# Relative bias added by VectorE in the band attention, and a new order of work around the second block's attentions

## The reference

```python
q = (u @ w_q).reshape(bsz, n_chunks, CHUNK, B_HEADS, B_HEAD_DIM)...
rel = jnp.clip(k_pos[None, :] - q_pos, -REL_CLIP, CHUNK - 1) + REL_CLIP
bias = rel_bias.astype(jnp.float32)[rel].transpose(2, 0, 1)
s = jnp.einsum('bqhd,bkhd->bhqk', qc, kb).astype(jnp.float32) * scale + bias
s = jnp.where(valid, s, MASK_VALUE)
p = jax.nn.softmax(s, axis=-1).astype(vb.dtype)
return jnp.einsum('bhqk,bkhd->bqhd', p, vb)
```

## Time and profile before

| | us |
|---|---|
| median of 3 runs | 1487.49 |
| lowest, highest | 1486.2, 1488.25 |
| profiled execution, its time | 1483.92 |
| profiled execution, its span | 1481.9 |
| PE busy | 1437.8 (97%) |
| DVE busy | 755.2 (51%) |
| ACT busy | 565.2 (38%) |

### The profile page before, as it was taken

How to read it: one execution, slowest core, us unless ns; L and a number is a source line. 1 busy time by engine, 2 the same in 40 slices (tenths; PEclk the granted TensorE clock), 3 DMA queues, 4 the chain that set the end, 5 groups by cost and what they waited for, 6 DMA issues and landing times. The chain is left out here.

```text
span 1481.9 us, 26323 instructions
## 1 busy us (share of the span) xinstructions
PE 1437.8 (97%) x11240; PEld 1211.5 (82%) x11240; DVE 755.2 (51%) x1194; ACT 565.2 (38%) x885; POOL 28.6 (2%) x47
## 2 busy tenths in 40 slices
PE   7999999999999999999999899999999999999997
PEld 4998899999999879999999789888666566566664
DVE  3968767876776656555555655644122122122121
ACT  2522235343454555444444664451212212212211
POOL 0100000000001010000000000010000000000000
PEclk9999999999999999999999999999999999999999
DMA  9996455979769514665645336426999999999996
GB/s 370 309 322 211 155 174 196 328 279 319 280 225 327 177 52 164 207 222 204 210 132 168 118 114 236 163 62 253 413 424 427 425 427 425 428 427 425 426 425 263
DMA packets 155378, 404.14 MB, mean 273 GB/s; under 512 B 5107, under 2 KB 123152, under 8 KB 133906
## 3 DMA queue, kind: packets, MB, share of 16 engines
q1 hardware_dynamic: 152960, 396.90, 71.1%
q0 software_dynamic: 1648, 5.18, 1.2%
q10 hardware_dynamic: 674, 0.64, 0.1%
HBM read 401.63 MB, written 1.07 MB: 272 GB/s over the span
## 5 line engine op out<-in xcount | busy, mean ns | idle before, releaser
L1999 PE MATMUL ps<-u,wsplit 128*128 128x256 f32 x3744 | 461.7, 284 | 5.3 <-DVE wsplit L1268 5.3
L1999 PEld LDWEIGHTS ps<-u,wsplit 128*128 128x128 f32 x3744 | 452.8, 192 | 11.9 <-DVE wsplit L1268 6.4
L1268 DVE TENSOR_TENSOR wsplit<-arena,wsplit 128x1024 fp32r<-128x1024 f32 x258 | 312.5, 1226 | 198.7 <-ACT wsplit L807 198.5
L807 ACT ACTIVATE wsplit<-arena 128x1024 fp32r<-128x1024 f32 x258 | 270.1, 1056 | 294.9 <-PE ps L1999 150.8
L2666 PE MATMUL ps<-arena 128*64 128x256 f32 x1408 | 155.9, 379 | 1.1 <-DVE arena L1897 0.8
L2666 PEld LDWEIGHTS ps<-arena 128*64 128x64 f32 x1408 | 101.6, 137 | 60.8 <-issue 12.6
L1902 DVE TENSOR_TENSOR arena<-arena,ps 128x256 f32<-128x256 f32 x32 | 13.5, 422 | 235.9 <-ACT arena L1216 223.8
L2261 PE MATMUL ps<-hid,wsplit 128*128 128x256 f32 x1056 | 130.7, 283 | 0.3 <-DVE hid L1524 0.3
L2261 PEld LDWEIGHTS ps<-hid,wsplit 128*128 128x128 f32 x1056 | 128.3, 192 | 0.5 <-DVE hid L1524 0.5
L1221 ACT ACTIVATE arena<-ps 64x512 f32<-64x512 f32 x62 | 36.6, 591 | 141.4 <-PE ps L2688 140.7
L2045 PE MATMUL ps<-wsplit,u 128*128 128x256 f32 x672 | 83.2, 284 | 1.8 <-ACT arena L1074 1.6
(11 more groups left out here) (369 smaller groups left out, 1376.3 us busy)
## 6 DMA issues: line engine op xcount, KB each, us to landing
arena<-in_w SPq DMA_DIRECT2D x64, 2048.0 KB, 22.4
late<-in_w SPq DMA_DIRECT2D x30, 2048.0 KB, 23.5
arena<-in_mod_w SPq DMA_DIRECT2D x48, 1024.0 KB, 7.0
arena<-in_ffn_w_in SPq DMA_DIRECT2D x44, 1024.0 KB, 5.9
arena<-in_ffn_w_out SPq DMA_DIRECT2D x22, 1024.0 KB, 5.0
arena<-in_a_w_in SPq DMA_DIRECT2D x16, 1024.0 KB, 8.6
arena<-in_kv_mod_w SPq DMA_DIRECT2D x8, 1024.0 KB, 4.9
arena<-in_kv_w SPq DMA_DIRECT2D x8, 1024.0 KB, 7.2
```

Of the source, the lines that this page charges most:

```text
L807: act.activation(piece_buf(p, 0), piece_src(p), ACT.Copy).then_inc(hi_done, 1)
L1268: dve.tensor_tensor(piece_buf(p, 1), piece_src(p), piece_buf(p, 0).bitcast(F32), ALU.subtract).then_inc(lo_done, 1)
L1999: mm = pe.matmul(o, w_[:, k, :], u[:, x_, k, :], start=first, stop=last)
```

## The change

Four things change. (1) In B the matmul with `flip` is gone, and with it POOL's two instructions that made `flip`. `qB` is written with the 128 queries of each block in reverse (`turned_back`), VectorE adds `biasB` to the scores out of PSUM into `sc_sb` before the maxima, the exponentials read `sc_sb`, and the two drains turn the queries back. A PSUM bank is now free for the next scores when the maxima are taken, not when the exponentials are. The waits for `biasB` move from TensorE to VectorE. (2) Ahead of W the memory operand's split is moved ahead of the last drain of `in2` and of one hi piece. (3) In W ScalarE and VectorE go head by head with their fillers, not pair by pair, and the drains of finished FILL pieces start one step sooner. (4) Three of the four reciprocals of `key_norm` move from `cq` to `out2`, and in X the probabilities of head 2 go ahead of the maxima of head 3, with the lo pieces of `co` one by one.

```diff
@@ attention_act
-                        src = sc_sb[:, i % 2, r] if kind == "W" else ps[:, 2 + i % 2, r]
+                        src = ps[:, 2 + i % 2, r] if kind == "X" else sc_sb[:, i % 2, r]
...
+                if kind == "W":
+                    for i in range(n + 3):
+                        if i < n:
+                            exps(i)
+                        if 2 <= i < n + 2:
+                            copy(i - 2)
+                        if i >= 4 and i % 2 == 0:
+                            drain(i - 3)
+                        if i >= 1:
+                            between(i - 1)
                     return
@@ queries, out_hi
-                act.activation(qB[:, 2 * n:2 * n + 2, :], bank(pair), ACT.Copy, scale=0.125).then_inc(lin_out["act"], 1)
+                act.activation(qB[:, 2 * n:2 * n + 2, :].rearrange("p c (b t) -> p (c b) t", b=TB),
+                               turned_back(bank(pair).rearrange("p c t -> p (c t)")), ACT.Copy, scale=0.125)\
+                   .then_inc(lin_out["act"], 1)
...
-                while 2 * drained[0] + 2 <= min(filled(min(i - 1, HW)), 14):
+                while 2 * drained[0] + 2 <= min(filled(min(max(i - 1, 0), HW)), 14):
@@ in2_act
                         act.activation(kdup, acc[:, 0:2, :], ACT.Copy).then_inc(w_dc, 1)
+                        hi_upto(pair[0]["w"] + LOOKAHEAD)
+                        memory_hi(pair[1]["w"])
...
                 if i == 0:
+                    hi_upto(FILL[3]["w"])
+                    wait_out(act, jobs["in2"][-1])
@@ add_gated
+                    if job == "out2" and n < 3:
+                        key_norm(n)
@@ attention_dve
+                    if kind == "B":
+                        dve.tensor_tensor(sc_sb[:, i % 2, every], src[:, every], biasB[:, i, :], ALU.add)\
+                           .then_inc(at_b, 1)
+                        dve.wait_ge(at_b, at + 1)
+                        src = sc_sb[:, i % 2, :]
...
                 if kind == "X":
                     scores(0)
                     for i in range(n + 2):
-                        if i == 1:
+                        if i in (1, 2):
                             probs(i)
                         if i + 1 < n:
                             scores(i + 1)
-                        if i < n and i != 1:
+                        if i < n and i not in (1, 2):
                             probs(i)
                         if i >= 2:
                             drain(i - 2)
                         between(i)
                     return
+                if kind == "W":
+                    for j in range(n // 2):
+                        scores(2 * j)
+                        scores(2 * j + 1)
+                        if j == 0:
+                            split_first()
+                        probs(2 * j)
+                        if j > 0:
+                            between(2 * j - 1)
+                        probs(2 * j + 1)
+                        between(2 * j)
+                    for i in (n - 1, n, n + 1):
                         between(i)
                     return
...
-                lambda i: lo_upto(jobs["co"][(1, 3)[i]]["w"]) if i < 2 else None)
+                lambda i: lo_upto(jobs["co"][1 + i]["w"]) if i < 3 else None)
@@ scores_two in attention_pe
-                        if i >= 2 and kind == "W":
+                        if i >= 2:
                             pe.wait_ge(at_b, before_b(a + m - 1))
-                        elif i >= 2:
-                            pe.wait_ge(at_e, 2 * (a + m - 1))
                         arriving(i + m)
-                        if bias:
-                            pe.matmul(o[m][:, 0:3 * P], flip, bias(i + m), start=True, stop=False)
```

54 lines of the change are left out of this document (29 added, 25 removed).

## The result

| | before | after |
|---|---|---|
| median beside each other, 4 executions each (us) | 1486.85 | 1463.3 |
| lowest, highest | 1479.72, 1488.25 | 1460.88, 1471.03 |
| ratio, 95% interval | | 0.9862, 0.982 to 0.9903 |
| executions that the means below rest on: count, mean | 62, 1482.3 | 23, 1466.7 |
| profiled execution: span, mean granted clock | 1481.9, 0.986 | 1469.0, 0.988 |

The 62 are later executions of the kernel before; the five first ones (1479.7 to 1488.3) are not among them, and with them the mean would be 1482.5. The 23 hold the five first ones of after.

What follows compares the result with a forecast made beforehand. Up to the experts TensorE's work and waits were taken as the bound, with the experts' DMA backlog moving along. Gains of 3.1 + 3.6 + 2.85 + 2.95 = 12.5 us from 1487.49 gave 1475 us, range 1468 to 1481.

Steps and rivals of the forecast that it cites:

- The bound, and what is kept: Up to the experts TensorE's work and waits set the time; savings ahead of 1033 us are kept one for one.
- Part 1, B -3.1: Stage B: removing bias matmuls saves 3.1 us, since VectorE becomes the bound at 4.7 us a pair instead of 5.23.
- the walk: Stage B: following one pair of heads step by step from its maxima through VectorE, ScalarE and TensorE, giving 4.7 us.
- Rival A: Stage B stays bound by TensorE and gives up to 11.0 us; sum 20.4, time 1467 us; chance 4%.
- Part 2, W -3.6: Ahead of and in W: five TensorE waits over a microsecond, 8.74 us in all, shrink or go, saving 3.6 us.
- Part 3, -2.85: key_norm and X: the 1.89 us wait for normed keys goes, head 2's turn comes 0.95 us sooner; 2.85 us together.
- The clock, -2.95: X: the half-clock stretch at 951.8 us goes with its wait, saving 2.95 us; two other stretches in W and X stay.
- The sum: Whole kernel: 3.1 + 3.6 + 2.85 + 2.95 = 12.5 us of gain.
- The reference: Whole kernel: gain taken from 1487.49 us, the median of three timed runs, giving 1475; the profiled execution was 1483.92.
- C: Gaps in B bring one or two half-clock stretches, the one at 951.8 stays; gain 7 us, 1480.5 us; chance 15%.
- D: TensorE at 1.2 GHz all through stage B: 21 us more there, 1496 us in all; chance 6%.
- E: Waits of W and X only move and B gives nothing: gain 0 to 3 us, 1486 us; chance 6%.

Runs made afterwards that it cites:

- order_only: Kernel before with the new orders ahead of and in W, in key_norm and in X, stage B keeping its bias matmuls; median 1467.45 us, ratio 0.989.
- after_2: The changed kernel run again without alteration, beside the kernel before; median 1465.44 us, ratio 0.9899 to the kernel before.
- mix_warm: Changed kernel with four matmuls that serve nothing in TensorE's 2.10 us wait in the first block's mixer; median 1465.95 us, ratio 0.9891.
- best_2: Second occasion of the changed kernel with stage B's fillers reordered and four useless matmuls in the mixer's wait; median 1464.39 us, ratio 0.9853.
- bias_only: Kernel before with only stage B changed: bias added by VectorE, queries reversed; median 1477.45 us, ratio 0.9971.
- w_only: Kernel before with only the new order ahead of and in stage W; median 1472.1 us, ratio 0.9925.
- before_warm: Kernel before with matmuls that serve nothing laid into three of TensorE's waits in W and X; median 1477.9 us, ratio 0.9985.
- x_only: Kernel before with only three key_norm reciprocals moved into out2 and the new order in X; median 1476.3 us, ratio 0.9957.
- add_twice: Changed kernel with every bias add in stage B done twice into the same place; its one execution took 1473.3 us.
- b_order: Changed kernel with another order of stage B's fillers, same work; median 1465.13 us, ratio 0.9904.
- best: Changed kernel with stage B's fillers reordered and four useless matmuls in the mixer's wait; median 1462.24 us, ratio 0.9874.

## Why the prediction was right or wrong

**The bound, and what is kept.** Right. The 425 us of the experts are as full as before, the chain ends with the same DMA, and what W and X saved arrived in the time of the executions (order_only). The row "experts" above is 3.0 us longer in after (472.1 for 469.1), by the stretch at half clock at 1007, ahead of the first expert.

**Part 1, B -3.1.** Right in mechanism and size for the stage; what it adds to the time beside the other parts is 0 to 1 us, as told above. From the maxima on, the walk holds to a tenth: set to the same start (after's stage B begins 1.70 us sooner), head 4's maxima stand at 512.73 (512.5 forecast), head 6's at 519.45 (519.44) and its turn at 522.50 (522.57). The period is 4.57 for 4.7. B was 2.8 us shorter in the profiled execution, and 3.8 in after_2, where no stretch at half clock fell in it. One number in it was wrong: TensorE's own work is 4.15 us a period, not "5.23 - 1.38" = 3.85. In after the scores start 0.48 us behind the turn (535.50 to 535.98), where the bias matmuls started 0.39 behind it (523.54 to 523.93); where the rest comes from was not looked into. For that the wait for P is 0.42, not the 0.85 of the forecast. It changed nothing on the time, since VectorE's chain was the bound either way. Rival A is refuted by the same rows.

**Part 2, W -3.6.** The mechanism was right, the size too small: the waits fell by 8.84 - 4.06 = 4.8. The terms left, forecast and measured: memory operand and first turn 1.75 and 1.65; gates 0.65 and none; copy of head 1 1.2 and 0.77; product of the gates 0.5 and 0.68; head 7's copy 1.25 and 0.96. All but the product of the gates were put too long, and that adds up to 1.3.

**Part 3, -2.85.** Right: 2.0 between W and X (1.89 forecast), and in X a wait of 1.23 for 2.13, 0.9 (0.95 forecast).

**The clock, -2.95.** This is the step that failed. "At the other two a wait of 1.2 and of 1.1 us remains, and I leave both falls in": the wait of 1.23 us in X remained, and no fall followed it in any of the 13 traces that have part 4. X took 55.3 or 55.4 us in all of them. In W none fell in the four traces of after; of all 13 traces with parts 2 and 3 six have one, which cost nothing in four (W 62.1) and 1.5 us in two (63.6, mix_warm and best_2). Between the two profiled executions the term was 6.3, not 2.95: 4.7 in X and 1.6 in W.

How much of the 6.3 is the change's is less sure, since before's trace was one draw. Over the three traces with an untouched X (before, bias_only, w_only) the clock cost 4.7, 1.7 and 1.6 us there, counted from the 56.25 of before_warm; over the three with an untouched W (before, bias_only, x_only) 1.5, 0 and 4.4, counted from 67.0. With 0.2 that remain in W on the mean of the 13 traces, the term is 4.4. The same three traces of W show that no rule for single waits could be read from one: in before only the wait of 1.39 had a fall behind it, so four of five had none (the prediction counts two), in bias_only the one of 2.10, in x_only those of 2.36 and 1.39. And the term priced no fall outside W and X: at 764 (2.7 us behind B by the landmarks) and at 1007 (3.0), after's trace has two, and the one at 764 has no wait ahead of it, against the prediction's "a wait is needed".

**The sum.** By the two profiled executions it is 2.8 + 4.8 + 2.0 + 0.9 + 6.3 = 16.8 us, and with 4.4 for the clock 14.9; between the means 15.6 were measured. So close an agreement is in part luck, since both sums leave out the stretches at 764 and 1007. Between the two profiled executions only 12.9 us appear, next to the 12.5 forecast, and that is chance: 16.8 less 2.7 and 3.0 for these two stretches, and 1.7 that after gained ahead of B. The full-clock yardstick gives the clock only 2.9 of 15.6 us because it sets the new stretches against the ones that went: in order_only, without part 1, the mean loss is 6.1 us under before's, in after 2.9.

**The reference.** "Against that median the forecast is 1475": I took 1487.49, the median of three, for the kernel's time, and 1483.92, the profiled execution, for one that ran 3.6 us fast. 62 executions have a mean of 1482.3, from 1476.4 to 1488.1: the three were high, the profiled one ordinary. From 1475 to the measured 1463.3 are 11.7 us. Of them 5.2 are this reference, 3.1 the gain (15.6 for 12.5), and 3.4 are chance: the four executions of the first comparison ran that much under after's mean of 1466.7. Counted from 1482.3, the forecast would have been 1469.8. Of the gain's terms W's waits (4.8 for 3.6) and the clock were too small, and the terms for B and X were not.

**The rivals.** C was half right: a stretch at half clock does come into B, and costs 1.0 us there (67.7 against 66.7), and others come behind B and behind X. But the one at 951.8 went with its wait. D, half clock all through B, did not occur: the gap of TensorE in each pair is 0.42, not 0.85, and behind these no fall followed in B in any trace. In add_twice, with a gap of 1.56 in each pair, TensorE was at half clock in two stretches of B (525.0 to 528.4 and 548.9 to 552.3) and at full clock in the rest. The Trainium skill's "TensorE: Matmul & The Clock Gate", section "What's actually happening", has activity release the clock; the traces agree as far as that a stretch came with the wait of 1.94 us in B in eight of the nine traces that have it (not in after_2), in b_order and best from 0.4 us before its end, and none with the waits of 0.42. The stretch at 764 speaks against a wait as its only cause. E did not happen.

## What to carry to other kernels

Before a forecast in tenths of a per cent, ask how much of the time is the granted clock's in that execution: one profile has one draw of it (the same X took 60.9, 57.9 and 57.8 us), and three executions are too few for a reference. When work is taken off TensorE at a place where another engine is close behind, the gain is the difference of the two chains (here 0.66 of 1.38 us a pair), and the new gaps can cost the clock; closing gaps gave more here (order_only, 14.7 us on the mean, all six executions within 3.4 us) than removing TensorE's work. Bound each wait that is left from both sides rather than late.

## What was not expected of the hardware

- The time at half clock varies between executions of one kernel by 10 us and more, and most of what two executions differ by follows it (correlation 0.93 over 62).
- A stretch at half clock can start without any wait of TensorE's: at 764 us in after, among matmuls of 128x2 and while TensorE is busy for 6.80 of 6.80 us. At the same matmuls before had none, and after_2 had none either. Ten of the 13 traces with parts 2 and 3 have a stretch there (761 to 771 us), and none of the four without; why, no run shows.
- A stretch can be free. In w_only, order_only, b_order and best one fell in W (in order_only at 838.4 to 841.8), with 1.7 us lost by the record, and W took 62.1 us as without it: in after TensorE waits for 0.77 and 0.68 us about there (840.9 and 842.5), and in these four it has neither wait. Windows of order_only, W's stretch, then X without any:

```profile
836.00:844.00 8.00, 8.00 (x62) 5.56 (x62) 7.51 (x21) 4.51 (x13) 0.00 (x0) 0.79 0.57 176
940.00:1000.00 60.00, 58.09 (x429) 55.11 (x427) 25.05 (x56) 28.29 (x54) 5.91 (x10) 1.00 0.41 147
```

- Reading 256 columns out of PSUM in reverse costs what a plain read does (0.42 us for the drain on VectorE, 0.37 on ScalarE, where the plain one took 0.39).
- What brings the falls exactly stays open: which of the waits of one to two microseconds are followed by one differs between kernels and between executions, and filling a wait moved the fall in one case, and four others had none in the one trace with them filled.
